# Context columns multiplied during two norms, adaLN pairs behind the tiles of down1, the root table loaded ahead

## What is computed

```python
x = x + rmsnorm(merged @ w_out[l], norm_mix_post[l])
h = rmsnorm(x, norm_ffn_pre[l])
u = causal_depthwise_conv(h @ w_ffn_up[l], ffn_conv_w[l], ffn_conv_b[l])
u_gate, u_val = jnp.split(u, 2, axis=-1)
y = (jax.nn.gelu(u_gate, approximate=True) * u_val) @ w_ffn_down[l]
x = x + rmsnorm(y, norm_ffn_post[l])
```

```python
m_lat = adaln_mod(c, w_mod[l], b_mod[l])        # silu(cond) @ w_mod + b_mod
m_ctx = adaln_mod(c_ctx, w_mod[l], b_mod[l])[None]
...
def ffn_sublayer(x, m, i, g, w_in, w_out):
    u = modulate(rms_norm(x, g), m, i)          # x * (1 + scale) + shift
    return x + 0.5 * m[:, 3 * i + 2][:, None] * swiglu(u, w_in, w_out)
```

## Time and profile before

| what | us |
|---|---|
| median of 3 runs | 2693.24 (2692.51 to 2696.74) |
| the profiled execution, its own time | 2692.29 |
| its span in the profile | 2690.5 |
| PE busy | 2580.0 |
| POOL busy | 1308.1 |
| DVE busy | 1406.1 |
| ACT busy | 1062.1 |

### The profile page before, as it was taken

One profiled execution on the slowest core, in us unless ns is written; L12 is line 12 of the kernel. 1 busy time (PEld: TensorE's weight loads), 2 busy tenths in 40 slices (PEclk: granted clock), 3 DMA queues, 4 the chain that ended last, 5 costly groups with the idle time before them and its releaser, 6 DMA issues.

```text
span 2690.5 us, 42350 instructions
## 1 busy us (share of the span) xinstructions
PE 2580.0 (96%) x14854; PEld 2237.4 (83%) x14854; DVE 1406.1 (52%) x3194; ACT 1062.1 (39%) x1937; POOL 1308.1 (49%) x654
## 2 busy tenths in 40 slices
PE   7998999979999999999999999999999999998997
PEld 7968989968888888867788888888888888788997
DVE  3665745555555662355466555665555443545221
ACT  4444457443222342256535222342222342565432
POOL 4605858654444444233344444444444453456875
PEclk9999989989999999999999999999999999999999
DMA  5605745553444543121233444544443452324553
GB/s 196 228 24 169 238 134 181 175 167 110 141 150 138 164 156 123 43 71 51 76 110 125 141 141 130 169 139 156 140 135 117 138 183 75 102 95 141 188 163 118
DMA packets 414006, 365.86 MB, mean 136 GB/s; under 512 B 7484, under 2 KB 412558, under 8 KB 413888
## 3 DMA queue, kind: packets, MB, share of 16 engines
q1 hardware_dynamic: 411448, 359.14, 41.7%
q10 hardware_dynamic: 2440, 5.16, 0.6%
HBM read 363.19 MB, written 1.08 MB: 135 GB/s over the span
## 4 chain that ended last, share of the span: by engine, by line
PE 68%; issue 14%; POOL 13%; DVE 2%; ACT 2%; DMA 0%; POOLq 0%; ACTq 0%; SPq 0%; DVEq 0%
PE bank L1921 56%; POOL w_lo L745 13%; PE bank L2412 2%; PE bank L2006 1%; PE bank L2007 1%; PE bank L2011 1%; PE bank L2452 1%; PE bank L2356 1%; DVE stat L1827 1%; PE bank L2132 1%; PE bank L2106 1%; PE bank L2133 1%; PE bank L2137 1%; PE bank L2348 1%; PE bank L2438 0%
## 5 line engine op out<-in xcount | busy, mean ns | idle before, releaser
L745 POOL TENSOR_TENSOR w_lo<-raw,w_hi 128x1024 fp32r<-128x1024 f32 (+2 forms) x602 | 1281.4, 2142 | 1279.4 <-ACT w_hi L816 792.3
L1921 PE MATMUL bank<-u_hi,w_hi 128*128 128x512 f32 (+1 forms) x2392 | 816.2, 341 | 4.2 <-POOL w_lo L745 2.5
L1921 PE MATMUL bank<-u_hi,w_lo 128*128 128x512 f32 (+1 forms) x2392 | 811.5, 339 | 0.0
L1921 PE MATMUL bank<-u_lo,w_hi 128*128 128x512 f32 (+1 forms) x2392 | 811.3, 339 | 0.0
L816 ACT ACTIVATE w_hi<-raw 128x1024 fp32r<-128x1024 f32 (+3 forms) x388 | 361.3, 947 | 891.3 <-PE bank L1921 712.7
L1921 PEld LDWEIGHTS bank<-u_hi,w_hi 128*128 128x128 f32 x2392 | 455.6, 190 | 74.8 <-issue 24.9
L1921 PEld LDWEIGHTS bank<-u_hi,w_lo 128*128 128x128 f32 x2392 | 455.4, 190 | 49.4
L1921 PEld LDWEIGHTS bank<-u_lo,w_hi 128*128 128x128 f32 x2392 | 455.6, 190 | 47.9
L1438 DVE SCALAR_TENSOR_TENSOR bank<-mod_raw,cond,bank 128x256 f32<-128x256 f32 x1008 | 401.1, 481 | 0.0
L1921 PE MATMUL bank<-hid_hi,w_hi 128*128 128x512 f32 (+1 forms) x880 | 309.2, 351 | 22.0 <-POOL w_lo L745 21.9
L1921 PE MATMUL bank<-hid_lo,w_hi 128*128 128x512 f32 (+1 forms) x880 | 307.4, 349 | 0.0
(11 more groups left out here) (270 smaller groups left out, 3468.0 us busy)
## 6 DMA issues: line engine op xcount, KB each, us to landing
raw<-in_ffn_w_in SPq DMA_DIRECT2D x88, 1024.0 KB, 5.0
mod_raw<-in_w_mod SPq DMA_DIRECT2D x144, 512.0 KB, 4.5
raw<-in_w_in SPq DMA_DIRECT2D x67, 1024.0 KB, 5.1
raw<-in_ffn_w_out SPq DMA_DIRECT2D x64, 704.0 KB, 4.6
raw<-in_w_ffn_up SPq DMA_DIRECT2D x22, 1024.0 KB, 5.0
raw<-in_w_ffn_down SPq DMA_DIRECT2D x16, 704.0 KB, 4.7
raw<-in_w_attn_out SPq DMA_DIRECT2D x8, 1024.0 KB, 5.1
raw<-in_w_o SPq DMA_DIRECT2D x8, 1024.0 KB, 5.0
```

Source lines behind the costliest of these rows:

```text
L745: pool.tensor_tensor(st.half(t, w_lo[slot]), st.half(t, raw[slot]), st.half(t, w_hi[slot]).bitcast(f32), ALU.subtract).then_inc(lo_ready, 1)
L1921: ins = pe.matmul(dst, s, v, start=first and n == 0, stop=final and n == 2)
```

## The change

Six things are edited. (1) The norm `n0_0` is no late norm any more, and its shift products, early tiles, scaling and `add_shift` are gone. (2) PE multiplies the context columns of blocks 0 and 1 of up_00, four tiles of 24 matmuls of 256 columns, beside the sums and spreads of the two norms, and then the latent columns of both blocks tile by tile as the normed input comes. (3) In down1 DVE works on the pair behind the body's two strips. (4) ACT picks the root table at the start of each `rows_gemm`. (5) In the last body of down1 the square of the last strip stands before both high parts that belong there; before it stood between them. (6) up_00 has no separate first body on ACT, so the table pick of its body 0 comes behind the normed tiles, in the loop.

```diff
-         mod_bodies=range(3), acc=2, shift=("n0_0", 1))
+         mod_bodies=range(3), acc=2)
...
+        if l == 0:
+            norm("n0_0", TO_U)
+            first = {}
+        else:
+            first = late_norm(f"n0_{l}")
...
@@ -862,6 +866,9 @@
                 tiles = st.acc
+                act.wait_ge(table_set, table_calls[0] + 1)
+                act.activation(table_pick[:, 0:1], eps[0:1, 0:1], ACT.Sqrt).then_inc(table_set, 1)
+                table_calls[0] += 1
...
-                            if last:
-                                tile(i, done, final)
+                            if final and c == st.per - 1 and t == (0 if nxt is None and st.per == 4 else 1):
+                                tile(i, c // 2 if st.per == 4 else done, final)
                             split_two_ahead(st, i, c, final, [t])
...
             mean_root("n_ffn_post", S, 1)
+            squares("n0_0", lambda k: x[:, k, S:T], lambda k: [(updated, KD + k + 1)])
+            mean_root("n0_0", S, KD)
             for k in range(KD):
-                act.wait_ge(updated, KD + k + 1)
-                act.wait_ge(early_lo, plan.at("n0_0", "early") + k + 1)
-                early_tile("n0_0", bass.ds(k, 1), bank[3])
-                act.activation(sq[:, k, :], x[:, k, S:T], ACT.Square).then_inc(sq_ready, 1)
+                act.wait_ge(xn_ready, plan.at("n0_0", "xn") + k + 1)
+                act.activation(u_hi[:, k, S:T], normed(k)[:, 0:S], ACT.Identity, bias=mod[:, k, LAT:LAT + 1]).then_inc(u_part, 1)
...
-                     first=late_first(f"n0_{l}", late_work(T), ACT.Silu, *sums, busy=base))
+                     first=late_first(f"n0_{l}", late_work(T), ACT.Silu, T, busy=base) if l else None)
...
@@ -1495,12 +1504,15 @@
-                        if st.per == 4:
+                        if st.per == 4 and name != "down1":
                             for pair, step in pairs[t:t + 1]:
                                 mod_pair(st, pair, step)
                         if final and st.whole and t == (0 if st.per == 2 else 1):
                             shift_products(st.shift)
                         tile(st, i, t, final)
+                    if name == "down1":
+                        for pair, step in pairs:
+                            mod_pair(st, pair, step)
...
-                    late_norm(st.late, st, late_work(w))
+                    if st.late is None:
+                        ada_norm("n0_0")
+                    else:
+                        late_norm(st.late, st, late_work(w))
...
             rows_gemm("down1", copy_y(4), context_rows)
-            shift_products("n0_0", 0, 4)
-            norm_x("n_ffn_post", "g_ffn_post", beside=lambda: shift_products("n0_0", 4, KD),
-                   then=lambda k: early_rest("n0_0", bass.ds(k, 1), k, bank[3]))
+            norm_x("n_ffn_post", "g_ffn_post")
...
@@ -2310,16 +2324,44 @@
-            column_sums("n_ffn_post", S)
-            spread("n_ffn_post", S)
             pe.wait_ge(u_ready, plan.at("ctx_norm", "u") + KD)
...
+            def halves_apart(st):
...
+                for c in range(2):
+                    for t in range(2):
+                        pe.wait_ge(lo_ready, st.parts(0, c, t))
+                        hidden_tile(KF)(st, 0, 2 * c + t)
+                        for k in range(KD):
+                            terms(c, t, k, slice(0, S))
+                            if (c, t, k) == (0, 0, 3):
+                                column_sums("n_ffn_post", S)
+                        if (c, t) == (0, 0):
+                            spread("n_ffn_post", S)
+                        if (c, t) == (1, 0):
+                            column_sums("n0_0", S, False, range(4))
+                column_sums("n0_0", S, False, range(4, KD))
+                spread("n0_0", S)
+                u0 = plan.at("n0_0", "u")
+                for k in range(KD):
+                    pe.wait_ge(u_ready, u0 + k + 1)
+                    latent(0, k)
+                    if k % 2 == 1:
+                        latent(1, k // 2)
+                for k in range(KD // 2, KD):
+                    latent(1, k)
```

More of the change, by code:

```diff
@@ L1333, in norm_u, with norm_x @@
                         lo_part(k - 1, normed(k - 1)[:, 0:S], u0, S, t0)
-            def norm_x(name, gain, dst=None, beside=None, then=None):
+            def norm_x(name, gain, dst=None):
                 x0, n0 = plan.at(name, "xn"), plan.at(name, "upd")
-                rstd_of(name, S, beside)
+                rstd_of(name, S)
                 for k in range(KD):
@@ L1385, in rest, with late_norm @@
                     ins.then_inc(u_ready, 1)
+                rstd_of(name, S * len(norm_halves(name)), take_shift)
+                for n in range(len(passes) + 1):
+                    if n < len(passes):
+                        norm(n)
+                    if n >= 1:
+                        rest(n - 1)
+                    if beside is not None and n == 5:
+                        beside()
+                dve.wait_ge(u_ready, u0 + len(passes))
+            def late_norm(name, st, late_tile):
+                sc0, turn = plan.at(name, "scaled"), before_joint(name).shift_turn
                 def take_shift():
@@ L1401, in scale, with scales @@
                     dve.tensor_tensor(dst, dst, bank[5][:, rows], ALU.mult).then_inc(scaled, 1)
[L1403 to L1412, removed]
+                def scales():
+                    scale(0)
+                    scale(1)
+                ada_norm(name, take_shift, scales)
                 dve.wait_ge(scaled, sc0 + 2)
@@ L1426, in clear_sums, with products @@
                 link(dve.memset(root[:, 0, :], 0.0))
-            def products(step, halves, src, by, final, first=0, last=KD):
-                for k in range(first, last):
+            def products(step, halves, src, by, final):
+                for k in range(KD):
                     for n, h in enumerate(halves):
@@ L1964, in gemm @@
                     late(st)
-                    body(0, ready, 1)
+                    if st.late is not None:
+                        body(0, ready, 1)
                     body(1)
@@ L1969, in gemm @@
                             body(i)
-                elif st.shift and st.bodies > 2:
+                elif (st.shift or final is not None) and st.bodies > 2:
                     with pe.Fori(0, st.bodies - 1) as i:
@@ L2312, in _, with terms, latent @@
             gemm("down1", down_strips(hid1_hi, hid1_lo, S, 0), final=lambda: spread("ctx_norm", S))
-            column_sums("n_ffn_post", S)
-            spread("n_ffn_post", S)
             pe.wait_ge(u_ready, plan.at("ctx_norm", "u") + KD)
[L2317 to L2322, removed]
+            def halves_apart(st):
+                def terms(c, t, k, cols):
+                    slot = (st.first + c) % 2
+                    at = slice(k * BLK + t * P, k * BLK + (t + 1) * P)
+                    return three(bank[2 * c + t][:, cols], w_hi[slot][:, at], w_lo[slot][:, at], u_hi[:, k, cols], u_lo[:, k, cols],
+                                 k == 0, k == KD - 1)
+                def latent(c, k):
+                    for t in range(2):
+                        ins = terms(c, t, k, slice(S, T))
+                        if k == KD - 1:
+                            ins.then_inc(group_done, 1)
+                for c in range(2):
+                    for t in range(2):
+                        pe.wait_ge(lo_ready, st.parts(0, c, t))
[11 more added lines that the diff above has]
+                u0 = plan.at("n0_0", "u")
+                for k in range(KD):
+                    pe.wait_ge(u_ready, u0 + k + 1)
[4 more added lines that the diff above has]
+                    latent(1, k)
             def layer(l):
```

25 lines of the change are left out of this document (9 added, 16 removed).

## The result

The changed kernel has a median of 2678.06 us over 4 runs (2674.83 to 2680.03), and 4 runs of the kernel before on the same chip have 2694.79 (2692.51 to 2696.74). The ratio is 0.9938, with an interval of 0.9925 to 0.9951: faster by 0.6%, about 17 us. The forecast was 2677.5. The profiled execution of the changed kernel is the slowest of its four, 2680.03 us with a span of 2678.2, so a difference between the two profiled executions (12.3 us) is smaller than that of the medians.

What follows compares the result with a forecast made beforehand. PE, busy for 96% of the span, was taken as the bound, so gains come where it waits or runs below full clock. 2692.29 less 13.0 and 2.7 gives 2676.6 us (2677.5 on the median's side); range 2671 to 2685.

Steps and rivals of the forecast that it cites:

- Pairs behind the tiles: In down1: three PE stalls go, bodies take 18.6 us, the last body stalls 9.6; down1 gains 3.8 us.
- The loads: In down1: a weight load lands after 4.75 us beside the pairs' loads, part of the loop setting 18.6 us bodies.
- A burst: Slower rival, chance 0.02: in down1 held-up loads come together and land in 7.7 us; time 2695 us.
- Context columns beside the norms: From down1 to up_00: block 2 starts at 612.9 in place of 625.89, 13.0 us including down1's 3.8.
- the gap: PE's wait between the sums of n0_0 and the first latent product at 601.1, put at 2.9 us.
- The slow start: Low PE clock behind the gap before up_00's latent half, 1 to 2 us, counted only in the loads rival.
- the rival in which the loads decide: Chance 0.24: raw landings of 5.3 to 5.5 us, down1 gains nothing, slow start; gain 10 us, time 2683.
- The root table: At the norms: picking the root table ahead saves 1.3 us behind w_out, 0.6, 0.5 and 0.3 elsewhere, 2.7 in all.
- The rival in which the table does not stay: Chance 0.05: the root set is loaded again at the root, 3.7 us are missing, time 2681 us.
- Sum: Whole kernel: 2692.29 less 13.0 and 2.7 gives 2676.6 us, or 2677.5 on the median's side.
- No rival: Four rivals: loads decide 0.24, last body doesn't stall 0.14, table doesn't stay 0.05, slower 0.02; central case 0.51.

Runs made afterwards that it cites:

- e3: Changed kernel with ACT's eight context tiles in down1's last body moved behind the high parts of blocks 2 and 3; 2674.12 us.
- e4: Changed kernel with DVE multiplying down1's pair 2 between the last body's two strips, behind the context rows; 2669.35 us.
- e9: Changed kernel with down1's pair loads cut to a quarter (512 to 128 KB), DVE's work the same; 2674.80 us.
- e10: Changed kernel with down1's weight loads cut to 5 of 11 row tiles; 2672.97 us.
- e5: Changed kernel with all eight sums of n0_0 ahead of the fourth context tile and the spread inside it; 2677.59 us.
- e6: Changed kernel with the edits of e4 and e5 together; 2666.69 us.
- e11: The changed kernel unaltered, timed again beside the kernel before; median 2676.14 us, ratio 0.9937 to before.
- the second set: Five rounds timing the kernel before (median 2691.83 us), e11 (2676.14) and e12 (2666.27) together.
- e12: The same kernel as e6, timed beside the kernel before; median 2666.27 us, ratio 0.9900 to before.

## Why the prediction was right

**Pairs behind the tiles.** The mechanism came as forecast: the three stalls went, bodies of 18.6 us (18.6, and 19.6 at a clock of 0.91), small waits of about 1 us inside them, one stall in the last body by the order pair, context rows, ACT's tiles, high part. DVE began the pair at 558.03 (forecast 553.5 and 4.7, 558.2), and PE went on at 572.08 (forecast 572.2). That these two agree so closely is luck in part: body 2 ended 1.2 us late (554.7 for 553.5), and DVE came to the pair only 3.4 us behind that end, not 4.7, which cancels it. The stall was 8.3 us for 9.6 because it began later, at 563.8 for 562.6. Down1's last matmuls ended at 581.8, forecast 582.2. e3 and e4 show the cause by taking either end of that order away.

**The loads.** Landings were 4.8 against the 4.75 assumed. A burst was feared for the pairs' halves; their median from 500 to 575 fell from 6.2 to 5.4 us. e9 shows that they do not pace down1, e10 that the weights' landing does.

**Context columns beside the norms.** The sums, the spread, the gap (2.6 us, forecast 2.9) and the start of the latent half at 601.1 are where they were put. One term was mis-sized: **the latent half was given 11.5 us at full clock and took 13.9** (601.11 to 615.00). At full clock it takes 11.9 (e5, e6), so the size that was wrong is in the main the clock's 2.0 us. The slow start was named, but only inside the rival in which the loads decide, at 1 to 2 us; it belonged into the central sum. So block 2 came at 615.0 and not at 612.9, and the gain up to there, from down1's first matmul, is 10.9 us instead of 13.0 (11.8 in e11, 125.9 less 114.05, where the clock of the first 5 us of the latent half was 0.66). A small part of the difference is a reading: 625.89 is where the chain's piece of the kernel before begins, and its timeline has block 2's first matmul at 625.73. The 0.124 us a matmul of that stretch in e5 is near the 0.12 that the rows gave; the 2.5 ns on top of the columns that the Trainium skill (TensorE: Matmul & The Clock Gate, section Wait — 56ns, not 53.3ns?) gives would make, as an estimate, 12.1 us of its 111 matmuls where they took 13.8.

**The root table.** Forecast were 1.3 us behind w_out, 0.6 at the end, 0.5 at `n2_0`. Behind w_out, from the first sum to up1's first matmul, 15.04 us became 13.35: 1.7 gained. At the end, from the last sum to the spread, 1.77 became 1.16: 0.6. At `n2_0` 2.98 became 2.29: 0.7. With 0.3 for the other four, the forecast's figure, that is 3.3 us for 2.7. The ten added loads (nine by the count, 14 to 23, since one goes) cost nothing that a view shows. The rival in which the table does not stay falls by the eight loads on the pick's line and none before a later root.

**Sum.** On the profiled executions 12.3 us were gained against 15.7 forecast. From down1's first matmul to block 2 the changed kernel is 10.9 us shorter, and from there to the end of the span 1.6 (of which 0.7 at `n2_0` and 0.6 at the end). The 1.7 us behind w_out do not show in this pair of executions, since the changed kernel came to that norm 2.5 us later (its first sum at 357.64 for 355.15; in e11 at 353.14), and both started down1 at almost the same time (499.99 and 499.84). The forecast had left the gain behind w_out out of its times around down1, so that these fit so well on the span's clock is luck too: in e11 the start of down1, the latent half and block 2 come 3.2 to 4.2 us sooner. By medians the gain is 16.7 and, in the second set, 15.7 us. The forecast of 2677.5 lies between the medians 2678.06 and 2676.14. No rival came true as a whole.

## What to carry to other kernels

A piece of work moved out of the way of one consumer lands in front of the next one of the same in-order engine, so its price is read at the first thing behind it that the bounding engine will ask for, through every engine that hands it on; here that was three engines away, and the one further move past the context rows was worth 7.1 us (115.0 less 107.9), more than the 4.6 of the move itself. Work with a late due time goes behind all of that. A chain of small sums, root and spread is best placed so that one filler tile is still left to multiply: that hides the chain (2.6 us here). The clock was kept with it in two profiled executions out of three. Where single executions differ by more than an edit is worth, measure from the last common instruction to the first one behind the edit.

## What was not expected of the hardware

The granted clock fell to 0.50 behind a gap in which PE stood for only 0.55 and 1.60 us, after sums of one column; it stayed so for about 5 us and cost 2.0 us. In the eight profiled executions with this gap the latent half took 13.1 to 14.1 us, with a clock of 0.50 to 0.69 at its start, against 11.9 at full clock. In the kernel before, PE stood for 0.55 and 1.33 us at the like place (611.91 to 614.73), with four such sums instead of sixteen ahead of it, and both windows from 609 to 619 have a clock of 1.00. Whether the gap or the sums bring the clock down is open. e5 and e6 have 32 sums in one run and no gap, and their clock stayed at 1.00; e12, the same kernel as e6, has them as well and no gap either, and its matmuls slowed down 0.7 us behind the last sum. So the rival of e5, in which the clock falls for the sums, is not excluded, and the same kernel can go either way.

The start of down1 varied by 5 us between programs that are the same up to there, and by 3.2 us between two executions of the changed kernel. And a loop that is entered with another table set loads its own in every body, here nine more loads of 1.28 us, at no cost that a view shows beside an ACT that is busy for 40% of the span.
